# A conditioned hybrid decoder block on one core: who splits the weights and the activation in the first stage

## The reference, cut to what matters

```python
mod = silu_c @ w_ada[l] + b_ada[l]                 # c is one row: six vectors of 2048
sh1, sc1, g1, sh2, sc2, g2 = jnp.split(mod, 6, axis=-1)
h = modulate(rms_norm(x, norm1_w[l]), sh1, sc1)    # rms_norm(x) * (1 + sc1) + sh1
proj = h @ w_in[l]                                 # 7168 columns: 8 retention and 8 attention heads
...                                                # the heads give `mixed` (512 x 2048)
x = x + g1[:, None, :] * mixed
h2 = modulate(rms_norm(x, norm2_w[l]), sh2, sc2)
mlp = jnp.square(jax.nn.relu(h2 @ w_mlp1[l])) @ w_mlp2[l]
x = x + g2[:, None, :] * mlp
return rms_norm(x, final_norm_w)
```

## Time and profile before

| what | before |
|---|---|
| median of 3 runs | 2533.4 us (2532.05 to 2536.89) |
| span of the profiled execution | 2531.9 us |
| PE busy, share of the span | 2393.8 us, 95% |
| DVE busy | 1320.0 us, 52% |
| ACT busy | 758.0 us, 30% |
| POOL busy | 290.0 us, 11% |
| end of the first stage (VectorE starts on the heads) | 191.8 us |

### The profile page before, as it was taken

One profiled execution on the slowest core, in us unless ns is written; L12 is line 12 of the kernel. 1 busy time (PEld: TensorE's weight loads), 2 busy tenths in 40 slices (PEclk: granted clock), 3 DMA queues, 4 the chain that ended last, 5 costly groups with the idle time before them and its releaser, 6 DMA issues.

```text
span 2531.9 us, 28560 instructions
## 1 busy us (share of the span) xinstructions
PE 2393.8 (95%) x10412; PEld 1939.1 (77%) x10412; DVE 1320.0 (52%) x1660; ACT 758.0 (30%) x1014; POOL 290.0 (11%) x170
## 2 busy tenths in 40 slices
PE   2778999999999999999999999999999999999996
PEld 2557778877777778778888888888888888888885
DVE  6988998995555553383333333333333333333344
ACT  3123333434344442242122232221221221222332
POOL 2542232231221210040000000000000000000000
PEclk9889999999999999999999999999999999999998
DMA  8776777772222242222232222222222222222222
GB/s 308 274 249 219 255 271 262 260 257 67 75 75 66 75 134 100 91 75 100 91 100 91 91 99 93 97 92 99 91 99 91 97 94 91 99 91 93 99 92 83
DMA packets 98309, 328.23 MB, mean 130 GB/s; under 512 B 10064, under 2 KB 18768, under 8 KB 98128
## 3 DMA queue, kind: packets, MB, share of 16 engines
q1 hardware_dynamic: 97248, 326.41, 37.8%
q10 hardware_dynamic: 1008, 1.13, 0.2%
HBM read 323.31 MB, written 4.19 MB: 129 GB/s over the span
## 4 chain that ended last, share of the span: by engine, by line
issue 63%; PE 23%; DVE 11%; ACT 2%; POOL 1%; DMA 0%; ACTq 0%; DVEq 0%; POOLq 0%
PE bank L355 6%; PE bank L356 6%; PE bank L359 6%; DVE ada_sb L827 5%; DVE prob L827 2%; PE bank L454 1%; DVE w_lo L820 1%; PE bank L392 1%; DVE hm L861 1%; ACT w_hi L575 1%; PE bank L394 0%; PE bank L393 0%; DMA prob<-mask_in 0%; PE bank L420 0%; PE bank L398 0%
## 5 line engine op out<-in xcount | busy, mean ns | idle before, releaser
L355 PE MATMUL bank<-act_hi,w_hi 128*128 128x512 f32 x2176 | 874.0, 402 | 63.7 <-DVE act_lo L865 56.9
L356 PE MATMUL bank<-act_lo,w_hi 128*128 128x512 f32 x2176 | 866.1, 398 | 0.0
L575 ACT ACTIVATE w_hi<-raw 128x1024 fp32r<-128x1024 f32 x400 | 422.4, 1056 | 961.2 <-PE bank L359 959.9
L820 DVE TENSOR_TENSOR w_lo<-raw,w_hi 128x1024 fp32r<-128x1024 f32 x383 | 489.2, 1277 | 405.1 <-ACT w_hi L575 392.1
L355 PEld LDWEIGHTS bank<-act_hi,w_hi 128*128 128x128 f32 x2176 | 421.3, 194 | 159.5 <-issue 65.3
L359 PE MATMUL bank<-act_hi,w_lo 128*128 128x512 f32 x2176 | 538.3, 389 | 0.0
L356 PEld LDWEIGHTS bank<-act_lo,w_hi 128*128 128x128 f32 x2176 | 420.9, 193 | 87.8
L359 PEld LDWEIGHTS bank<-act_hi,w_lo 128*128 128x128 f32 x2176 | 408.8, 188 | 85.2
L355 PE MATMUL bank<-u_hi,w_hi 128*128 128x512 f32 x1024 | 407.0, 397 | 0.0
L356 PE MATMUL bank<-u_lo,w_hi 128*128 128x512 f32 x1024 | 405.9, 396 | 0.0
L1157 DVE SCALAR_TENSOR_TENSOR xy<-bank,modr,xy 128x512 f32 (+1 forms) x144 | 108.1, 751 | 456.9 <-PE bank L359 456.9
(11 more groups left out here) (129 smaller groups left out, 1324.6 us busy)
## 6 DMA issues: line engine op xcount, KB each, us to landing
raw<-weights SPq DMA_DIRECT2D x400, 512.0 KB, 3.2
ada_sb<-ada SPq DMA_DIRECT2D x172, 512.0 KB, 4.5
prob<-ada SPq DMA_DIRECT2D x20, 512.0 KB, 4.1
xy<-x_t SPq DMA_DIRECT2D x16, 512.0 KB, 6.4
out<-xy SPq DMA_DIRECT2D x4, 1024.0 KB, 9.1
decay_sb<-decay SPq DMA_DIRECT2D x7, 256.0 KB, 4.1
silu_c<-c_row SPq DMA_DIRECT2D x1, 1024.0 KB, 5.6
rot_sb<-rot ACTq DMA_DIRECT2D x2, 256.0 KB, 5.9
```

The source lines that it names most:

```text
L355: pe.matmul(acc[:], stationary, hi, start=first, stop=False)
L356: pe.matmul(acc[:], stationary, lo, start=False, stop=False)
L575: nc.scalar.activation(w_hi[:, w], raw[:, r], ACT.Copy).then_inc(hi_ready, 1)
L820: nc.vector.tensor_tensor(w_lo[:, w], raw[:, r], w_hi[:, w].bitcast(F32), ALU.subtract).then_inc(lo_ready, 1)
```

## The change

Five things change.

1. In the first stage `normed` moves from GpSimd to VectorE and takes the scale along: one fused operation makes `hf` = x * `amul` * `r_all`. ScalarE then only adds the shift. `hm` is gone: `act_lo` is made in one fused operation from `hf`, the shift and `act_hi`. The same holds for the second norm (n = 1).
2. The low halves of the first 17 weight chunks are made by VectorE instead of GpSimd. GpSimd keeps one small operation in the stage, the root.
3. The k tiles go in groups (0), (1, 2), (3, 4), ... (13, 14), (15) instead of pairs (0, 1), (2, 3), ... (14, 15).
4. Within VectorE's list the eight dots of the next group are dealt out around the work of this group: two between `normed` and `modulated_rest`, six behind the weights' low halves. The first dots stand between the steps of the mean and the root. The copies of `ident` move behind the sums of squares and the copy of `mask` into group 1, so that the sums no longer wait for the load of the mask.
5. ScalarE rounds chunk k + 2 behind the `modulated_hi` of k's group.

```diff
+K_GROUPS = ((0,),) + tuple((k, k + 1) for k in range(1, KT - 1, 2)) + ((KT - 1,),)
...
 # ScalarE
-                nc.scalar.activation(act_hi[:, k], hf[:, k % 2], ACT.Identity, bias=shift,
-                                     scale=amul[:, n, k:k + 1]).then_inc(act_hi_ready, 1)
+                nc.scalar.activation(act_hi[:, k], hf[:, k % 2], ACT.Identity, bias=shift).then_inc(act_hi_ready, 1)
...
-            modulated_hi(0, 0, 1)
-            modulated_hi(0, 1, 1)
-            for p in range(KT // 2):
-                round_w(Count(2 * p + 1))
-                round_w(Count(2 * p + 2))
-                if p < KT // 2 - 1:
-                    modulated_hi(0, 2 * p + 2, p + 2)
-                    modulated_hi(0, 2 * p + 3, p + 2)
-                if p == 4:
+            round_w(Count(1))
+            for g, ks in enumerate(K_GROUPS):
+                for k in ks:
+                    modulated_hi(0, k)
+                for k in ks:
+                    if k + 2 <= FIRST:
+                        round_w(Count(k + 2))
+                if g == 5:
                     act.wait_ge(lam_dotted, 1)
                     nc.scalar.activation(lam_exp[:], lam_sum[:], ACT.Exp).then_inc(lam_exped, 1)
...
 # VectorE
+            def normed(n, k):
+                dve.wait_ge(scale_ready, GROUP_OF[k] + 1 if n == 0 else len(K_GROUPS) + 1)
+                dve.wait_ge(r_all_ready, n + 1)
+                if k >= 2:
+                    dve.wait_ge(act_ready, 2 * KT * n + k - 1)
+                nc.vector.scalar_tensor_tensor(hf[:, k % 2], xy[:, k], amul[:, n, k:k + 1], r_all, ALU.mult, ALU.mult)\
+                    .then_inc(hf_ready, 1)
...
-                nc.vector.tensor_scalar(hm[:, k % 2], hf[:, k % 2], amul[:, n, k:k + 1], shift, ALU.mult, ALU.add)\
-                    .then_inc(hm_ready, 1)
-                dve.wait_ge(hm_ready, KT * n + k + 1)
                 dve.wait_ge(act_hi_ready, 2 * KT * n + k + 1)
-                nc.vector.tensor_tensor(act_lo[:, k], hm[:, k % 2], act_hi[:, k].bitcast(F32), ALU.subtract)\
-                    .then_inc(act_ready, 1)
+                nc.vector.scalar_tensor_tensor(act_lo[:, k], hf[:, k % 2], shift, act_hi[:, k].bitcast(F32),
+                                               ALU.add, ALU.subtract).then_inc(act_ready, 1)
...
-            dve.wait_ge(ident_landed, 16)
-            dve.wait_ge(mask_landed, 16)
-            nc.vector.tensor_copy(ident_r[:], ident[:])
-            nc.vector.tensor_copy(ident_b[:], ident[:]).then_inc(const_ready, 1)
-            nc.vector.tensor_copy(mask[:], mask_f).then_inc(setup_ready, 1)
             for m in range(KT):
                 sum_square(m)
...
+            for g, ks in enumerate(K_GROUPS):
+                dots = [(k, e) for k in (K_GROUPS[g + 1] if g + 1 < len(K_GROUPS) else ()) for e in range(4)]
+                for k in ks:
+                    normed(0, k)
+                for k, e in dots[:2]:
+                    dots1(k, e)
+                for k in ks:
+                    modulated_rest(0, k)
+                for k in ks:
+                    rest_w(Count(k))
+                for k, e in dots[2:]:
+                    dots1(k, e)
+                if dots:
+                    modulation1(g + 1)
...
 # GpSimd
-            def normed(n, k):
...
-            def rest_w(s):
...
```

More of the change, by code:

```diff
@@ L306, in _ @@
                 sp.dma_start(xy[:, 2 * p:2 * p + 2], x_t[:, 2 * p:2 * p + 2]).then_inc(x_landed[p], 16)
-            for p in range(KT // 2):
-                for a in range(8 * p, 8 * p + 8):
+            for k in range(KT):
+                for a in range(4 * k, 4 * k + 4):
                     load_ada(Count(a))
-                    if a % 8 in (2, 5):
-                        load_raw(Count(2 * p + (a % 8) // 4))
+                    if a % 4 == 2:
+                        load_raw(Count(k))
             load_raw(Count(FIRST))
@@ L828, in dot_ada, with dots1 @@
                                                1.0, 0.0, ALU.mult, ALU.add, to).then_inc(dot_done, 1)
[L830 to L841, removed]
+            def dots1(k, e):
+                dot_ada(Count(4 * k + e), part1[:, k, e // 2, e % 2:e % 2 + 1])
@@ new lines, in modulation1 @@
+            def modulation1(g):
+                ks = slice(K_GROUPS[g][0], K_GROUPS[g][-1] + 1)
+                n = len(K_GROUPS[g])
+                dve.wait_ge(dot_done, 4 * ks.stop)
+                nc.vector.tensor_tensor(sum1[:, 0:n], part1[:, ks, :, 0], part1[:, ks, :, 1], ALU.add).then_inc(mod_summed, 1)
+                dve.wait_ge(mod_summed, g + 1)
+                bias = vec[:, V_B1 + 2 * ks.start:V_B1 + 2 * ks.stop].rearrange("p (a b) -> p a b", b=2)
+                nc.vector.tensor_tensor(mod1[:, ks], sum1[:, 0:n], bias, ALU.add).then_inc(mod_ready, 1)
+                dve.wait_ge(mod_ready, g + 1)
@@ L1070, in _ @@
             nc.vector.tensor_scalar(inv_hd[:], ones[:], 1.0 / HD, None, ALU.mult).then_inc(const_ready, 1)
-            dve.wait_ge(ident_landed, 16)
-            dve.wait_ge(mask_landed, 16)
-            nc.vector.tensor_copy(ident_r[:], ident[:])
-            nc.vector.tensor_copy(ident_b[:], ident[:]).then_inc(const_ready, 1)
-            nc.vector.tensor_copy(mask[:], mask_f).then_inc(setup_ready, 1)
             for m in range(KT):
                 sum_square(m)
-            token_scale(1)
+            dve.wait_ge(ident_landed, 16)
+            nc.vector.tensor_copy(ident_b[:], ident[:])
+            nc.vector.tensor_copy(ident_r[:], ident[:]).then_inc(const_ready, 1)
             dve.wait_ge(vec_landed, 16)
             dve.wait_ge(silu_ready, 1)
-            modulation1(0)
-            modulated_rest(0, 0)
-            modulated_rest(0, 1)
-            for p in range(KT // 2):
-                if p < KT // 2 - 1:
-                    modulation1(p + 1)
-                    modulated_rest(0, 2 * p + 2)
-                    modulated_rest(0, 2 * p + 3)
-                if p == 3:
+            dots1(0, 0)
+            token_mean(1)
+            dots1(0, 1)
+            token_diag(1)
+            dots1(0, 2)
+            dots1(0, 3)
+            modulation1(0)
+            for g, ks in enumerate(K_GROUPS):
[12 more added lines that the diff above has]
+                    modulation1(g + 1)
+                if g == 1:
+                    dve.wait_ge(mask_landed, 16)
+                    nc.vector.tensor_copy(mask[:], mask_f).then_inc(setup_ready, 1)
+                if g == 4:
                     dve.wait_ge(lam_landed, 16)
@@ L1174, in _ @@
                     sum_square(KT + m)
-            token_scale(2)
-            modulated_rest(1, 0)
-            modulated_rest(1, 1)
+            token_mean(2)
+            token_diag(2)
+            for k in range(2):
+                normed(1, k)
+            for k in range(2):
+                modulated_rest(1, k)
             for j in range(8):
                 if j < 7:
-                    modulated_rest(1, 2 * j + 2)
-                    modulated_rest(1, 2 * j + 3)
+                    for k in range(2 * j + 2, 2 * j + 4):
+                        normed(1, k)
+                    for k in range(2 * j + 2, 2 * j + 4):
+                        modulated_rest(1, k)
                 rest_w(Count(C_MLP + j + 1))
@@ L1313, in _ @@
             token_root(2)
-            for k in range(KT):
-                normed(1, k)
             token_root(3)
```

61 lines of the change are left out of this document (20 added, 41 removed).

## The result

| | before | after |
|---|---|---|
| median of the runs | 2532.99 us (4 runs, 2532.05 to 2536.89) | 2503.46 us (4 runs, 2502.71 to 2507.70) |
| ratio | | 0.9882, 95% interval 0.9868 to 0.9896 |
| span of the profiled execution | 2531.9 us | 2501.5 us |
| VectorE / GpSimd busy over the span | 1320.0 / 290.0 us | 1284.5 / 185.0 us |
| first stage ends (VectorE on the first head) | 191.81 us | 163.35 us |

A forecast was written before the change was run, and what follows sets the result against it. VectorE, held up by GpSimd, bounds the first stage. The stage saves 29.7 us, the second norm 1.5, together 31.2: 2531.9 - 31.2 = 2500.7, with 1.5 to the median 2502 us; range 2492 to 2514 us.

The forecast's parts named there:

- VectorE stands still while GpSimd works on SBUF: First stage: a pair's eight dots take 15.7 us against 9.1 undisturbed; 6.6 us of standing still go.
- The rival that the dots are long for the DMA writes' sake: First stage: dots are long because of DMA writes into SBUF, so the 6.6 us stay; 2543 us, chance 0.04.
- Durations of the added work: VectorE, first stage: fused hf and act_lo 0.67 us each, w_lo 1.13 us start to start; 14.8 us a group.
- The rival of half throughput: First stage: fused operations on two non-bf16 SBUF sources run at half throughput; 16.7 us a group, 2511 us, chance 0.05.
- The ring at 2.7 us: Between first-stage groups TensorE idles for one rounding, act_hi, act_lo and signals, 2.7 us; 13.6 or 16.2 us a turn.
- Start: Before the first chunk: sums end at 23.0 instead of 25.35 us, TensorE starts at 34.0 instead of 44.12 us.
- some 1.2 us: Between the sums and r_all: the root's wait for GpSimd's first low half, some 1.2 us, goes.
- Groups and the 2 us beside them: First stage from 46.9 us: six groups of 15.3 us, plus 2 us for mask copy, lambda's products and Exp.
- Last pair and last chunk: End of the first stage: last pair 12.2 us, gap 2.7, last chunk 6.5; stage ends at 162.1 us.
- DMA at nothing: First-stage loads, 5.2 MB a group, 354 GB/s in 14.8 us, cost nothing; the contrary rival 2509 us, chance 0.11.
- The second norm at 1.5 us: From r_all of the second norm, TensorE starts at about 1081.6 instead of 1083.06 us, 1.5 us less.
- The heads at nothing: Behind the first stage everything keeps its order, so the 29.7 us saved stay; the contrary rival has chance 0.04.

The follow-up runs named there:

- a_wlo_pool: The changed kernel with the low halves of the first 17 weight chunks back on GpSimd and nothing else; 2521.48 us, ratio 0.9950.
- p_two: The changed kernel plus 12 useless GpSimd subtractions of two 128 x 1024 SBUF tensors in the first stage; 2528.45 us, ratio 0.9976.
- p_one: The changed kernel plus 12 useless GpSimd multiplications by a constant, reading one 128 x 1024 SBUF tensor, in the first stage; 2511.18 us, ratio 0.9906.
- after_again: The changed kernel run and profiled once more, nothing altered; 2507.01 us, ratio 0.9887.
- b_norm2: The kernel before, with hf and the fused low half on VectorE for the second norm alone; 2534.53 us against 2534.43, ratio 0.9998.
- b_start: The kernel before, with only the ident copies behind the sums of squares and the mask copy behind the first pair; 2534.55 us against 2534.43, ratio 0.9997.
- a_ring_open: The changed kernel with ScalarE's rounding that waits for a group's last chunk put behind the next group's act_hi; 2497.32 us, ratio 0.9851.

## Why the prediction was right

Forecast 2502 us, measured 2503.46. Point by point, in the order of its steps:

- **VectorE stands still while GpSimd works on SBUF.** Right, and shown in both directions: by taking away (the dots at 1220 ns), by undoing (a_wlo_pool), by doing each part alone, and by adding (p_two, p_one). The prediction charges only VectorE for it; GpSimd is held beside VectorE as well (see the start). The rival that the dots are long for the DMA writes' sake is dead: the loads run faster now (317 against 271 GB/s) with dots of 1.22 us.
- **Durations of the added work.** Right: 748 ns for both fused operations and 0.67 us from one to the next (two take 1.41 us), 1219 ns for `w_lo`. The rival of half throughput (2511 us) is refuted for these operands: 748 ns against 692 for a plain subtraction of the same tile.
- **The ring at 2.7 us.** Right in mechanism and size (2.70 us). What the clock does in it was left open and is a mixture as assumed: some groups begin at 1.2 GHz (row 63.70 to 67.10 us, 0.58), others begin at full clock and fall to 1.2 GHz a microsecond later, and the last pair stays at full clock. The three turns from 64.85 us on are 12.5 to 12.8 us of TensorE and the gap, 15.2 to 15.5 us; the two of 17.0 and 16.1 us hold the Exp and follow it.
- **Start.** The sums end at 23.04 us (forecast 23.0) and `r_all` begins at 30.33. TensorE starts at 35.35 instead of 34.0, and the term that was mis-sized is the root's: "some 1.2 us" of waiting for GpSimd were taken off, but the root takes 0.84 us longer beside a dot, and from the end of the sums to the end of `r_all` it is 7.9 us as before. Of the rest, 0.34 us are the late chunk 1 and some 0.2 us signals. Group 1 starts 1.5 us late by this, at 48.36.
- **Groups and the 2 us beside them.** From group 1 to the last pair it is 95.4 us, not 93.8. The 15.3 us a group with the allowance for the Exp were 1.6 us too little over six groups.
- **Last pair and last chunk.** 19.6 us instead of 21.4; from 132 to 157 us the granted clock is 0.99. This takes back 1.8 of the 3.1 us above, and it is luck: in after_again the same stretch has the lower clock at its start and takes 23.8 us. The stage ends at 163.35 us, forecast 162.1.
- **DMA at nothing.** Right here; no dot waits for a row. With the ring open the queues are at 0.93 of their time and 344 GB/s, and VectorE, busy 99.10 of 100 us, still does not wait for rows.
- **The second norm at 1.5 us.** Mis-sized: from `r_all` to TensorE 1.18 us less. And 0.96 us are given back: from TensorE's start to `tok_v` at the end it is 1430.31 us instead of 1429.35. Half of that (0.49 us) falls in the first two chunks, where the granted clock over the first 20 us is 0.86 instead of 0.88; where the other half goes stays open. b_norm2 shows gain and give-back by themselves.
- **The heads at nothing.** From the stage end to the `amul` of the second norm it is 374.43 us instead of 376.16, 1.73 less that no step had foreseen. Other kernels with the same heads took from 374.5 to 379.3 us, and the kernel after itself 377.21 us in after_again, so this is within what that stretch varies by; what it varies with stays open.

The sum: 28.5 + 1.7 + 1.2 - 1.0 = 30.4 us of span, 31.2 forecast. The misses of a microsecond or two have both signs; that the total fits to 1.5 us is partly luck, that the stage fits to 1.3 us mostly so too: the same kernel profiled again has its stage end 2.2 us later.

## What to carry to other kernels

Before giving GpSimd elementwise work "because it is idle", look at what VectorE's instructions last beside it: here 2.5 us of GpSimd work on two tensors cost VectorE 2.2 us, while VectorE would have done it in 1.13. Then draw the ring that the new order makes: an instruction that waits for the last work of a group, put ahead of what starts the next group in an in-order queue, costs its whole tail every turn, and moving it behind was worth 6 to 8 us of this kernel (by the medians and by the ratios). A gain ahead of a stretch in which TensorE is the bound and its clock is low may come back only in part.

## What the runs showed of the hardware

- A GpSimd operation with one SBUF source also holds VectorE, for less: a dot loses 0.84 us beside a multiplication of 128 x 1024, against 2.2 us beside a subtraction of two. The expectation had either all of it or nothing.
- It is not only VectorE's two-source operations: in b_start the copy of the mask, which has one source, lasts 2.40 us beside a `w_lo` of GpSimd (44.23 us), and 0.22 us without in the kernel before.
- GpSimd pays too: a subtraction of this size, 1.22 us on VectorE, takes GpSimd 2.34 us with VectorE idle (b_start at 25.15 us) and 3.06 us on average in p_two, and the root grows from 1.02 to 1.86 us beside a dot. The multiplication took 3.30 us on average.
- Behind a gap of 2.7 us the clock was lower in most groups, and not always at once: the group at 64.85 us runs at 0.58 until 67.10 us, that at 80.00 us begins at full clock and runs at 0.51 from 81.24 to 84.57 us, and that at 143.79 us, behind the same gap, stays at 1.00. In a_ring_open the groups behind gaps of 0.95, 2.06 and 2.03 us took 11.2 us, so they ran at full clock throughout.
- The queues of one core moved 413 GB/s in the stretch from 63.70 to 67.10 us and 317 over the whole stage, with VectorE, ScalarE and TensorE at work.
